# Stick-breaking attention moved between the steps around it, in a two-block transformer on one core

## What is computed

```python
def swa_sb_mixer(h, positions, w_in, w_out, q_norm, k_norm, sinks):
    qa, ka, va, qb, kb, vb = jnp.split((h @ w_in).astype(f32), cuts, axis=-1)
    ...   # qa, ka: head norms, rope
    out_a = sliding_window_attention(qa, ka, va, sinks)   # 8 heads, 2 key groups
    out_b = stick_breaking_attention(heads_b(qb), heads_b(kb), heads_b(vb))   # 8 heads
    return jnp.concatenate([out_a, out_b], axis=-1) @ w_out

def stick_breaking_attention(q, k, v):
        z = q . k * HEAD_DIM ** -0.5
        log_fail = jnp.where(causal, -jax.nn.softplus(z), 0.0)
        log_after = lax.cumsum(log_fail, axis=3, reverse=True) - log_fail
        a = jnp.where(causal, jnp.exp(jax.nn.log_sigmoid(z) + log_after), 0.0)
        out = a . v
```

## Time and profile before

| | us |
|---|---|
| median of 3 runs | 2410.12 (2408.43 to 2411.41) |
| the profiled execution | 2409.01 |
| its span | 2407.1 |
| end of the last `ab_in` slot | 72.39 |
| first product of `ab_out` | 123.74 |
| first mask product of the nsa softmax | 1275.07 |
| first product of `nsa_out` | 1340.09 |

### The profile page before, as it was taken

One profiled execution on the slowest core, in us unless ns is written; L12 is line 12 of the kernel. 1 busy time (PEld: TensorE's weight loads), 2 busy tenths in 40 slices (PEclk: granted clock), 3 DMA queues, 4 the chain that ended last, 5 costly groups with the idle time before them and its releaser, 6 DMA issues.

```text
span 2407.1 us, 37033 instructions
## 1 busy us (share of the span) xinstructions
PE 2329.9 (97%) x15383; PEld 2112.7 (88%) x15383; DVE 1894.5 (79%) x2094; ACT 1346.4 (56%) x1320; POOL 2.4 (0%) x8
## 2 busy tenths in 40 slices
PE   9899999999999999999998899999999999999997
PEld 9699999999999999999997778888888888888886
DVE  6786896887877969554567579988998989898897
ACT  5555333454453334433426357776777677777775
POOL 0000000000000000000000000000000000000000
PEclk9999999999999999999999999999999999999999
DMA  6143454542434454455331259999999999999995
GB/s 254 53 174 124 143 187 179 184 141 106 149 141 140 177 187 162 170 177 191 136 115 40 71 218 374 374 360 344 359 376 358 346 358 376 357 343 358 374 360 218
DMA packets 163415, 556.85 MB, mean 231 GB/s; under 512 B 8752, under 2 KB 8880, under 8 KB 124976
## 3 DMA queue, kind: packets, MB, share of 16 engines
q1 hardware_dynamic: 162048, 547.45, 62.2%
q10 hardware_dynamic: 1008, 6.49, 0.7%
q0 software_dynamic: 192, 0.52, 0.1%
HBM read 552.86 MB, written 1.05 MB: 230 GB/s over the span
## 4 chain that ended last, share of the span: by engine, by line
PE 70%; DVE 3%; ACT 3%; issue 1%; DMA 1%; DVEq 0%; ACTq 0%; SPq 0%
PE ps L1648 12%; PE ps L1650 12%; PE ps L1649 12%; PE ps L1019 8%; PE ps L1021 8%; PE ps L1020 8%; PE ps L1156 2%; ACT whi L561 1%; PE ps L1099 1%; PE ps L1414 1%; PE ps L1627 1%; DMA raw<-stream 1%; DVE wlo L1807 0%; PE ps L1694 0%; DVE x L2668 0%
## 5 line engine op out<-in xcount | busy, mean ns | idle before, releaser
L1807 DVE TENSOR_TENSOR wlo<-raw,whi 128x2048 fp32r<-128x2048 f32 x519 | 1186.9, 2289 | 256.1 <-ACT whi L561 195.5
L561 ACT ACTIVATE whi<-raw 128x2048 fp32r<-128x2048 f32 x519 | 993.7, 1916 | 573.3 <-PE ps L1021 350.0
L1019 PE MATMUL ps<-hh,whi 128*128 128x256 f32 x2080 | 596.6, 287 | 11.5 <-DVE hl L1902 7.1
L1020 PE MATMUL ps<-hl,whi 128*128 128x256 f32 x2080 | 591.1, 284 | 0.0
L1021 PE MATMUL ps<-hh,wlo 128*128 128x256 f32 x2080 | 590.9, 284 | 0.0
L1019 PEld LDWEIGHTS ps<-hh,whi 128*128 128x128 f32 x2080 | 401.9, 193 | 14.5 <-DVE hl L1902 7.2
L1020 PEld LDWEIGHTS ps<-hl,whi 128*128 128x128 f32 x2080 | 402.0, 193 | 0.4
L1021 PEld LDWEIGHTS ps<-hh,wlo 128*128 128x128 f32 x2080 | 401.7, 193 | 0.0
L1648 PE MATMUL ps<-whi,hh 128*128 128x512 f32 x896 | 358.2, 400 | 2.0 <-DVE hl L2619 2.0
L1650 PE MATMUL ps<-wlo,hh 128*128 128x512 f32 x896 | 350.8, 392 | 0.0
L1649 PE MATMUL ps<-whi,hl 128*128 128x512 f32 x896 | 349.6, 390 | 0.0
(11 more groups left out here) (359 smaller groups left out, 2668.9 us busy)
## 6 DMA issues: line engine op xcount, KB each, us to landing
raw<-stream SPq DMA_DIRECT2D x519, 1024.0 KB, 5.5
work<-w_in ACTq DMA_DIRECT2D x1, 2240.0 KB, 8.7
stage<-stage_consts ACTq DMA_DIRECT2D x4, 512.0 KB, 4.1
work<-mem_in ACTq DMA_DIRECT2D x2, 1024.0 KB, 5.8
x<-x_in SPq DMA_DIRECT2D x1, 1024.0 KB, 4.9
out<-x SPq DMA_DIRECT2D x4, 256.0 KB, 2.3
const<-consts SPq DMA_DIRECT2D x1, 548.5 KB, 9.4
work<-work POOLq DMA_DIRECT2D x4, 128.0 KB, 2.7
```

The lines of the kernel that those rows point to most:

```text
L561: nc.scalar.activation(whi[hi_at(g, odd)][:, :], raw[g % RAWS][:, :], ACT.Copy).then_inc(hi_ready, 1)
L1019: mm(out_ap, hi_w, hi_x, start=start, stop=False, **kw)
L1020: mm(out_ap, hi_w, lo_x, start=False, stop=False, **kw)
L1807: V.tensor_tensor(wlo[g % RAWS][:, :], raw[g % RAWS][:, :], whi[hi_at(g, odd)][:, :].bitcast(F32), ALU.subtract).then_inc(lo_ready[g % RAW ...
```

## The change

The stick-breaking scores, their masks and the exponentials of |z| and the ln move beside the last four slots of `ab_in` (the ln and the fourth unit's chain just behind them); running sums and subtractions stand in the four sliding steps, products with the values in the four steps after. Two input slots swap places (`AB_SLOTS`) so that the operands are there in time. Of each head's 512 score columns the 128 that the causal mask empties are left out, so 768 columns a unit stay of 1024. PSUM is divided anew: stick-breaking uses banks 6 and 7 throughout, the sliding scores banks 0 and 1 or half of banks 4 and 5, the outputs the other halves. The load of the exp table ahead of the sliding softmax, the second copy of its masks and the zero products around the running sums are gone. The flags that let `ab_out` start come in parts. In the shared helpers the transposes and the value products stand one step later than before, the maxima of nsa are negated by the reduction itself, the cross attention's take one more small operation, and four scalings become one operation.

```diff
+        sb_t = over("sb_t", "ahi", 1536, skip=2048)
...
+        AB_SLOTS = (0, 1, 2, 3, 5, 4, 6, 7, 8)
...
-        SB_T = [Wc(4608 + 1024 * i, 1024) for i in range(4)]
-        SB_Z = [sb_z[:, 1024 * i:1024 * (i + 1)] for i in range(3)] + [W(14, 4)]
+        SB_KEPT = BLK + P
+        SB_T = [sb_t[:, 2 * SB_KEPT * i:2 * SB_KEPT * (i + 1)] for i in range(2)] + [Wc(4608 + 2 * SB_KEPT * i, 2 * SB_KEPT) for i in range(2)]
+        SB_Z = [sb_z[:, 2 * SB_KEPT * i:2 * SB_KEPT * (i + 1)] for i in range(4)]
+        by_head = lambda t: t.rearrange("p (h c) -> p h c", h=2)
+        in_banks = lambda: banks(6).rearrange("p (h c) -> p h c", h=2)[:, :, 0:SB_KEPT]
...
+        def scores_of(kind, u, nk):
+            if kind == "swa" and u % 2 == 0:
+                return r3(banks(4)[:, BLK:BLK + 512], 4)
+            return r3(banks(0 if kind == "swa" else SCORE_BANK[u % 2]), 4)[:, :, 0:nk]
+        def sliding_out(o):
+            return ps[:, 4, 0:BLK] if o % 2 == 0 else ps[:, 5, BLK:512]
...
-                if kind != "nsa":
-                    load_exp()
...
             def sb_small(u):
                 act.wait_ge(z_masked, u + 1)
+                act.wait_ge(heads_ready, 1) if u == 2 else None
                 link(nc.scalar.activation(SB_T[u], SB_Z[u], ACT.Abs))
-                nc.scalar.activation(SB_T[u], SB_T[u], ACT.Exp, scale=-1.0).then_inc(sb_exp, 1)
-            softmax_act("swa", SWA_U, {u - 1: lambda u=u: sb_small(u) for u in range(4)})
-            for u in range(4):
-                act.wait_ge(sb_exp, u + 1)
+                link(nc.scalar.activation(SB_T[u], SB_T[u], ACT.Exp, scale=-1.0))
                 nc.scalar.activation(SB_T[u], SB_T[u], ACT.Ln, bias=1.0).then_inc(soft_ready, 1)
-            for u in range(4):
+            def sb_weights(u):
                 act.wait_ge(d_ready, u + 1)
-                at_least(act, sb_pv_done, u - 1)
-                nc.scalar.activation(PT[u % 2], SB_Z[u], ACT.Exp).then_inc(a_ready, 1)
+                nc.scalar.activation(SB_T[u], SB_Z[u], ACT.Exp).then_inc(a_ready, 1)
+            split_phase("ab_in", {0: first_rstd, 1: sines, 3: swa_rstd, **{5 + u: lambda u=u: sb_small(u) for u in range(3)}})
+            softmax_act("swa", SWA_U, {-1: lambda: sb_small(3), **{1 + u: lambda u=u: sb_weights(u) for u in range(4)}})
             xa_act(0, "ab_out")
...
+                        scores = scores_of(kind, u, nk)
...
-                        for _ in range(2 if kind == "swa" or step < 3 else 1):
+                        for _ in range(2 if kind == "nsa" and step < 3 else 1):
...
-                    if 2 <= step <= len(us) + 1:
-                        u = u0 + step - 2
-                        if kind == "nsa" and step == 2:
+                    if 3 <= step <= len(us) + 2:
+                        u = u0 + step - 3
+                        if kind == "nsa" and step == 3:
                             pe.wait_ge(v_copied, 10)
...
-                    if step >= 3:
-                        u = u0 + step - 3
-                        g, qt, br = us[step - 3]
-                        o = o0 + (step - 3) // branches
+                    if step >= 4:
+                        u = u0 + step - 4
+                        g, qt, br = us[step - 4]
+                        o = o0 + (step - 4) // branches
...
-                        if br == 0:
+                        if kind == "swa":
+                            pe.wait_ge(exp_done, u0 + 3)
+                            at_least(pe, o_drained, sliding_drained(o - 2))
+                        elif br == 0:
...
-                at_least(pe, z_masked, u - 1)
+                pe.wait_ge(banks_drained, 5 if u < 2 else 7)
+                at_least(pe, z_masked, u)
                 for h in range(2):
                     rows = slice(64 * h, 64 * h + 64)
                     for kt in range(2):
-                        last = mm(ps[:, sb_bank(u) + h, kt * 256:(kt + 1) * 256], W(10 + u)[rows, kt * P:(kt + 1) * P], W(6 + u)[rows, :],
-                                  start=True, stop=True)
+                        last = mm(ps[:, 6 + h, kt * 256:kt * P + 256], W(10 + u)[rows, kt * P:(kt + 1) * P],
+                                  W(6 + u)[rows, kt * P:BLK], start=True, stop=True)
                 last.then_inc(z_ready, 1)
...
+            def sb_running_sums(u):
+                pe.wait_ge(sp_ready, u + 1)
+                if u == 0:
+                    pe.wait_ge(z_masked, 4)
+                else:
+                    pe.wait_ge(d_ready, u)
+                for h in range(2):
+                    lo_t, hi_t = SB_T[u][:, h * SB_KEPT:h * SB_KEPT + BLK], SB_T[u][:, h * SB_KEPT + BLK:(h + 1) * SB_KEPT]
+                    mm(ps[:, 6 + h, 0:BLK], C("ge"), lo_t, start=True, stop=False, skip_group_check=True)
+                    mm(ps[:, 6 + h, P:BLK], C("ones"), hi_t, start=False, stop=True, skip_group_check=True)
+                    last = mm(ps[:, 6 + h, BLK:SB_KEPT], C("ge"), hi_t, start=False, stop=True, skip_group_check=True)
+                last.then_inc(cs_ready, 1)
...
+            def sb_products(u):
+                pe.wait_ge(a_ready, u + 1)
+                if u < 2:
+                    pe.wait_ge(d_ready, 4)
+                else:
+                    pe.wait_ge(o_drained, breaking_drained(u - 2))
+                for h in range(2):
+                    for kt in range(2):
+                        last = mm(ps[64 * h:64 * h + 64, 6 + u % 2, kt * P:BLK], Wc(9728 + kt * 512 + (2 * u + h) * 64, 64),
+                                  SB_T[u][:, h * SB_KEPT + kt * BLK:h * SB_KEPT + BLK + kt * P], start=(kt == 0), stop=(kt == 1), skip_group_check=True)
+                last.then_inc(sb_pv_done, 1)
...
+            def after_ab_slot(s):
+                if s == 3:
+                    swa_sums()
+                if s == 7:
+                    swa_key_copies()
+                if s >= 5:
+                    sb_scores(s - 5)
+                if s == 5:
+                    swa_half_turns()
...
             softmax_pe("swa", SWA_U, SWA_O,
                        lambda g, h, qt: W(2 * g + h // 2)[64 * (h % 2):64 * (h % 2) + 64, qt * P:(qt + 1) * P],
                        lambda g, h, br: W(35 + g)[64 * (h % 2):64 * (h % 2) + 64, :],
                        lambda g, h, kt, br: Wc(9472 + kt * P + g * 64, 64),
-                       between={0: lambda: sb_scores(2), 1: lambda: sb_scores(3), 2: lambda: pe.wait_ge(z_masked, 3),
-                                3: lambda: pe.wait_ge(z_masked, 4)})
-            keep_warm(7, 8)
...
+                    drain(ph, s, lambda bank, s: V.scalar_tensor_tensor(
+                        out=r3(W(2 * AB_SLOTS[s], 2), 2), in0=r3(ps[:, bank, :], 2), scalar=64 ** -0.5 if AB_SLOTS[s] in (3, 4) else 1.0,
+                        in1=rstd[:, :].unsqueeze(1).to_broadcast([P, 2, BLK]), op0=ALU.mult, op1=ALU.mult))
...
+                largest = V.tensor_reduce(small[:, s0:s0 + 4], scores, AX, ALU.max, negate=True)
+                if kind == "nsa":
+                    largest.then_inc(negmax_ready, 1)
+                    return
+                link(largest)
+                link(V.scalar_tensor_tensor(out=small[:, s0:s0 + 4], in0=small[:, s0:s0 + 4], scalar=score_scale(kind),
+                                            in1=small[:, 632 + 4 * g:636 + 4 * g], op0=ALU.mult, op1=ALU.min))
+                V.tensor_tensor(small[:, s0 + 8:s0 + 12], small[:, s0:s0 + 4], R("sinks", 4 * g, 4), ALU.add).then_inc(negmax_ready, 1)
...
-                for h in range(4):
-                    ins = V.tensor_scalar(pr[:, h * 256:h * 256 + nk], pr[:, h * 256:h * 256 + nk],
-                                          small[:, s0 + 16 + h:s0 + 17 + h], None, ALU.mult)
-                ins.then_inc(probs_ready, 1)
+                part = r3(pr, 4)[:, :, 0:nk]
+                V.tensor_tensor(part, part, small[:, s0 + 16:s0 + 20].unsqueeze(2).to_broadcast([P, 4, nk]), ALU.mult).then_inc(probs_ready, 1)
...
+                    if st >= 4:
+                        u = u0 + st - 4
+                        g, qt, br = us[st - 4]
+                        if kind == "swa":
+                            sliding_kept(st - 4)
+                        elif br == branches - 1:
+                            o = o0 + (st - 4) // branches
...
+            def sliding_kept(u):
+                dve.wait_ge(pv_done, u + 1)
+                evacuate((2 * (u // 2), 2), (u % 2) * P, sliding_out(u))
+                dve.wait_ge(sb_pv_done, u + 1)
+                evacuate((4 + u, 1), 0, ps[:, 6 + u % 2, :], BLK)
+                if u % 2:
+                    dve.wait_ge(o_drained, sliding_drained(u))
+                    V.memset(small[:, 639:640], 0.0).then_inc(h_ready, 1 if u == 1 else 2)
+                if u == 3:
+                    dve.wait_ge(o_drained, breaking_drained(u))
+                    V.memset(small[:, 638:639], 0.0).then_inc(h_ready, 1)
...
             def sb_masked(u):
                 dve.wait_ge(z_ready, u + 1)
```

(29 more changed lines are left out.)

150 lines of the change are left out of this document (48 added, 102 removed).

## The result

| | before | after |
|---|---|---|
| median, us | 2410.09 (4 runs) | 2376.89 (2375.07 to 2378.11, 4 runs) |
| ratio | | 0.9854, 95% interval 0.9842 to 0.9867 |
| the profiled execution, its span | 2409.01, 2407.1 | 2378.11, 2376.2 |

The forecast was 2381 in a range of 2375 to 2391. The median lies inside the range and 4 us under the forecast. The same kernel was timed twice more, in other sessions: 2380.3 with a ratio of 0.9871 (0.9852 to 0.9890), and 2380.5 with 0.9875 (0.9854 to 0.9897). So the place and the sign were right, one term of the sum (B) was too small, and the lower end of the range had no room left for what the forecast did not know.

A forecast was written before the change was run, and what follows sets the result against it. PE bounds the kernel, busy 2329.9 of 2407.1 us, so only its waits can pay. 2409.0 - 20.9 - 0.3 - 8.0 = 2379.8, plus 1.1 for the runs' median, rounded to 2381; range 2375 to 2391.

The forecast's parts named there:

- term B: ACT's tables and layer 0's cross attention: table loads go, with little of PE's waiting; gain 0.3 us, at most 1.4.
- end of the last slot: `ab_in`: three score units beside its slots put 2.35 us on their end, so the last slot ends at 74.74.
- from there to the first maxima: Layer 0's attention: DVE's drain, copies, mask and softplus after the last `ab_in` slot take 4.6 us.
- DVE's four steps: Layer 0's attention: four sliding steps paced by DVE, of 2.8, 4.3, 3.5 and 3.4 us, together 14.0.
- PE's tail: End of layer 0's attention: sliding values, stick-breaking products, transposes and a bank wait on PE take 7.5 us.
- stand for the third block: Start of `ab_out`: after its first two blocks PE stands 0.6 us for the third, waiting on DVE's small copies.
- term A: Layer 0's attention: the rebuilt chain lets weight products run on from 102.8 instead of 123.74; gain 20.9 us, bounds 16.5 to 22.5.
- term C: nsa softmax: period of four units falls from 14.72 to about 13.0 us; gain 8.0 us, bounds 3 to 9.
- rival of the single pair of banks: Sliding steps: stick-breaking sums wait for subtractions in banks 6 and 7, adding 6.4 us, total 2387; chance 0.08.
- rival that DVE would bind: nsa softmax: DVE or two hops between engines pace it, so nsa gives only 3 us, total 2386; chance 0.08.
- The clock: Layer 0's attention without zero products: PE's clock falls to half, costing 8 to 10 us, total about 2390; chance 0.12.
- The splits' rival: `ab_in`: the slots' splits queue behind stick-breaking work, costing up to 34 us, total 2415, slower; chance 0.03.

The follow-up runs named there:

- a_again: The changed kernel, unaltered, timed again in five rounds beside the kernel before: 2380.34 us against 2410.89, ratio 0.9871.
- a_pe_more: Changed kernel plus eight products of zeros behind the running sums of each sliding step: first product of `ab_out` at 105.23 us, 2.4 later.
- a_best: Changed kernel with the second stick-breaking weights ahead of ACT's first copy of transposed probabilities, and copies of v moved from DVE to ACT: 2378.20 us, ratio 0.9862.
- a_behind: Changed kernel with all four stick-breaking scores, masks, |z|, exp and ln behind the last `ab_in` slot: `ab_out` starts at 109.95 us, 7.1 later.
- a_xa_exp: Changed kernel with the exp table loaded once behind the sliding softmax's last copy: slot 2 to the cross attention's last scores takes 80.91 us, against 79.23.
- b_tables: Kernel before, without the exp table load ahead of the sliding softmax, nothing else changed: ratio 0.9993 (0.9981 to 1.0004).
- b_nsa_step: Kernel before, with only nsa's transposes and value products one step later on PE, and outputs on DVE: ratio 0.9974, 6.3 us faster.
- b_warm: Kernel before, with products of zeros in PE's waits in sliding softmax and nsa: `ab_out` starts at 122.27 us, 1.47 sooner; nsa takes 65.46.

## Where the prediction held, and the term that was mis-sized

**The step that failed** is term B: 0.3 us, with bounds of 0 to 1.4, for the cross attention behind ACT's tables, where 1.7 us were measured. With it goes the lower end of the range, which allowed nothing for the clock in the parts that the change leaves alone. The mechanism of each term was right; what follows takes them one by one.

| step of the prediction | forecast | measured |
|---|---|---|
| end of the last slot | 74.74 | 75.52 |
| from there to the first maxima | 4.6 | 4.4 |
| DVE's four steps | 14.0 | 14.1 |
| from there to the first sliding values | 1.4 | 1.0 |
| PE's tail | 7.5 | 7.8 |
| stand for the third block | 0.6 | 0.3 |
| term A | 20.9 | 20.4 |
| term B | 0.3 (0 to 1.4) | 1.7 |
| term C | 8.0 (3 to 9) | 8.3, 6.8 in `a_again` |
| sum | 29.2 | 30.4 located, 30.9 by the spans |

**Term A** held step by step. The step that was most off is the lengthening of `ab_in`: a score unit takes 0.93 us and not 0.83, and there was no pause between slots that took some of it in, so the slots end 3.1 us later than before and not 2.35. The rival of the single pair of banks (6.4 us more for the four steps) did not come: DVE's steps took 14.1 us and hold one gap of 0.17. What I took for DVE's bound is one of DVE and PE with ACT between them (`a_pe_more`). That did not change the sum, since I had followed all three lists, but my sentence that both others fit beneath DVE was too strong, and `a_best` lives on the rest. What the runs do not separate is the share of each edit in the 20.4 us: the placement beside the slots is worth 7.1 (`a_behind`), and the rest is divided among sums and weights between the sliding units, the emptied quarter of the columns, the two table loads and the zero products, none of which was taken back alone on the changed kernel.

**Term B** was mis-sized, and its measured value lies outside my bounds: 1.7 us, all of it the table (`a_xa_exp`, `b_tables`). I had looked at one wait of PE, the one of 1.10 us, and left out the one of 1.12 us ahead of the head sums at 177.76. That one is gone whole, 42.44 us of the stretch becoming 41.16, and the other shrank from 1.10 to 0.76. I took 0.3 because DVE releases PE there. DVE in its turn stood behind ACT's table loads: `a_xa_exp`, which brings them back and nothing else, brings both waits back, at 1.12 and 1.10 us. I had not asked DVE's rows what DVE waited for.

**Term C** came out at its forecast for the reason given: the step later puts scores ahead of the transposes, and a period goes to 12.86 (forecast 13.0), PE's own work. The rival that DVE would bind fell with `b_nsa_step`, where even the heavier DVE work of before fits. Part of the 8.3 is luck with the clock: in `a_again` a stretch at 0.81 to 0.85 took 1.5 back, and nsa of before has its own window at 0.66.

**The clock** is where the argument had the wrong sign. I held it for a danger of the change (0.12). In the changed kernel's attention it read 1.00 in each of the three traces of it, without the zero products. It is the order of before that suffers: 1.3 to 1.5 us in its own trace (`b_warm`), 1.1 more in that of `b_nsa_step`. With the waits closed, the falls of the clock there are gone too. I had counted the 1.5 us only in the upper bound of A's gain.

**The splits' rival**, the one that ended slower, did not come: ACT's split behind the last |z| stands at 75.62, and PE waited for no split in `ab_in`.

**The range.** Its lower end was 2381 less 6. It had room for B's 1.1 above its value, A's 1.6 and C's 1.0, but nothing for the unchanged nine tenths of the kernel (1058 and 1067 us), which move by some 2 us each up or down between executions and make the median of four runs uncertain by as much. Most of that movement goes with the clock. The record has the mean granted clock of each execution. In 23 executions of the kernel before, the nine at 0.991 and 0.992 took 2405.7 to 2409.3 us, the ten at 0.989 and 0.990 took 2409.3 to 2413.8, and the four below took 2413.9 to 2417.9: some 1.9 us for each 0.001. All four executions behind the first median of the changed kernel had 0.993; of the eight of the two later sessions two had that, and took 2377.6 and 2379.5, while the six at 0.991 and 0.992 took 2377.8 to 2382.8. So the first median was in the scatter's lower part, and by those 1.9 us the clock would account for some 2 of the 3.5 us between the sessions, an estimate; the rest stays open. The two later medians of 2380.3 and 2380.5 stand within 1 us of the forecast. Luck has a part in that, since the sum was 1.2 us below the located gain and a median moves by more than that.

The same figures say that the change gains by the clock as well. Its mean is 0.990 in those 23 executions and 0.992 in the twelve of the changed kernel, 0.0025 more before rounding; at 1.9 us for each 0.001 that is some 5 us of the whole gain, an estimate from these runs. The 1.5 us of the attention and the window at 0.66 in nsa are part of it.

## What to carry to other kernels

In a chain of short pieces on three engines, write down each engine's list with durations and follow it. Sums of the operations on one engine gave wrong signs for small edits here, and the followed lists gave 20.9 for 20.4. When a wait names an engine, ask what that engine waited for before you price the wait. And put short, early work of a later stage beside the dense products of the one before: it was worth 7.1 us here, with the 3.1 us already paid that it puts on that stage. When two medians of one kernel differ, compare the granted clocks of their executions before looking for a cause in the kernel.

## What the runs showed of the hardware

- TensorE's granted clock fell without any long wait: in `a_behind` it went from 1.00 (72 to 75) to 0.50 (from 76 on) behind waits of 0.78 and 1.23 us with 0.93 us of products between them, while in the changed kernel waits of 0.93, 0.39, 1.16 and 0.64 us between stretches of 2.9 to 5.9 us of work left it at 1.00. Products of zeros in the waits kept it at 1.00, which bought 1.3 to 1.5 us in `b_warm`.
- The same order of instructions can meet the lower level at other moments: sixteen 64x256 products took 2.07 us in the trace of before and 3.73 in that of `b_tables`, where PE's list and its two waits ahead of them (0.79 and 1.70 us) were the same.
- In a kernel that keeps PE busy for 97% of the time the scatter between executions goes with the granted clock: in 23 executions of the kernel before, 0.986 to 0.992 went with 2417.9 to 2405.7 us.
- Choosing the table set once, ahead of a stage, decides on loads far behind it: with its preload at 74.42 the kernel before has eight loads of 1.28 us from 137.5 to 195.3, and without the preload (`b_tables`) it has none of the eight.
